# 64 bytes further: the FFN output units' split weights and the hT tiles in SBUF

## The reference

```python
def swiglu_2(h, w_in, w_out):
    a, b = jnp.split(h @ w_in, 2, axis=-1)
    return (jax.nn.silu(a) * b) @ w_out

def second_block(...):
    for l in range(DEPTH_2):
        h = rms_norm_2(x, ffn1_norm_pre[l])
        x = x + 0.5 * rms_norm_2(swiglu_2(h, ffn1_w_in[l], ffn1_w_out[l]), ffn1_norm_post[l])
        ...
        y = token_mixer(h, mem, ...)
        x = x + rms_norm_2(y, mix_norm_post[l])
        h = rms_norm_2(x, ffn2_norm_pre[l])
        x = x + 0.5 * rms_norm_2(swiglu_2(h, ffn2_w_in[l], ffn2_w_out[l]), ffn2_norm_post[l])
    return x
```

## Time and profile before

| | |
|---|---|
| median of three runs | 1726.48 us |
| the profiled execution | 1726.28 us |
| its span, first to last instruction | 1724.5 us |
| TensorE (PE) busy | 1717.4 us |
| VectorE (DVE) busy | 1072.7 us |
| ScalarE (ACT) busy | 918.9 us |
| matmuls | 12536 |
| granted clock of TensorE | full (1.00) |

### The profile page before, as it was taken

The page is one execution under the profiler, slowest core; times in us unless marked ns, Lnnn a source line. Parts: engine busy times, 40 slices in busy tenths (PEclk is TensorE's granted clock), DMA queues, the critical chain, the costliest instruction groups (busy, mean ns, idle before and its releaser), DMA issues.

```text
span 1724.5 us, 31112 instructions
## 1 busy us (share of the span) xinstructions
PE 1717.4 (100%) x12536; PEld 1586.4 (92%) x12536; DVE 1072.7 (62%) x1523; ACT 918.9 (53%) x1258; POOL 34.5 (2%) x60
## 2 busy tenths in 40 slices
PE   9999999999999999999999999999999999999998
PEld 9999888999999999999999999899999899989997
DVE  6555787655665566557677555755574667775555
ACT  6444677434454346577746444644464577664443
POOL 0000120000000000000000000000000000000000
PEclk9999999999999999999999999999999999999999
DMA  9655533655665555463355555655555553446552
GB/s 341 237 193 193 183 112 149 229 185 193 223 226 187 189 194 202 177 220 139 133 197 197 193 187 197 230 205 193 189 203 188 181 195 136 162 160 228 185 194 96
DMA packets 48415, 328.58 MB, mean 191 GB/s; under 512 B 5584, under 2 KB 5840, under 8 KB 10192
## 3 DMA queue, kind: packets, MB, share of 16 engines
q1 hardware_dynamic: 45504, 316.93, 51.3%
q10 hardware_dynamic: 2832, 10.54, 1.7%
HBM read 326.39 MB, written 1.05 MB: 190 GB/s over the span
## 4 chain that ended last, share of the span: by engine, by line
PE 99%; issue 0%; DVE 0%; ACT 0%; DVEq 0%; POOLq 0%; POOL 0%
PE work L1888 20%; PE work L1890 20%; PE work L1889 20%; PE acc L1890 8%; PE acc L1889 8%; PE acc L1888 8%; PE work L2129 4%; PE work L1993 3%; PE acc L2197 1%; PE acc L2251 1%; PE work L1978 1%; PE acc L2225 1%; PE acc L2215 0%; PE work L2379 0%; PE work L2259 0%; PE work L1950 0%
## 5 line engine op out<-in xcount | busy, mean ns | idle before, releaser
L1262 DVE TENSOR_TENSOR lo<-raw,hi 128x2048 fp32r<-128x2048 f32 x267 | 611.1, 2291 | 308.3 <-ACT hi L711 307.9
L711 ACT ACTIVATE hi<-raw 128x2048 fp32r<-128x2048 f32 x267 | 511.2, 1915 | 370.7 <-PE work L1890 346.8
L1888 PE MATMUL work<-xT_hi,hi 128*128 128x256 f32 x2464 | 685.4, 278 | 0.0
L1889 PE MATMUL work<-xT_lo,hi 128*128 128x256 f32 x2464 | 681.2, 276 | 0.0
L1890 PE MATMUL work<-xT_hi,lo 128*128 128x256 f32 x2464 | 681.1, 276 | 0.0
L1888 PEld LDWEIGHTS work<-xT_hi,hi 128*128 128x128 f32 x2464 | 462.6, 188 | 4.5 <-issue 1.7
L1889 PEld LDWEIGHTS work<-xT_lo,hi 128*128 128x128 f32 x2464 | 463.2, 188 | 2.4
L1890 PEld LDWEIGHTS work<-xT_hi,lo 128*128 128x128 f32 x2464 | 462.7, 188 | 0.0
L1890 PE MATMUL acc<-hi,hT_lo 128*128 128x512 f32 x480 | 189.1, 394 | 0.0
L1889 PE MATMUL acc<-lo,hT_hi 128*128 128x512 f32 x480 | 188.2, 392 | 0.0
L1888 PE MATMUL acc<-hi,hT_hi 128*128 128x512 f32 x480 | 186.4, 388 | 0.0
(11 more groups left out here) (357 smaller groups left out, 2108.0 us busy)
## 6 DMA issues: line engine op xcount, KB each, us to landing
raw<-stream SPq DMA_DIRECT2D x295, 1024.0 KB, 4.8
mem_in<-mem ACTq DMA_DIRECT2D x3, 1024.0 KB, 5.2
post<-post ACTq DMA_DIRECT2D x6, 512.0 KB, 4.4
raw<-stream SPq DMA_DIRECT2D x4, 512.0 KB, 9.3
memT_raw<-mem2T ACTq DMA_DIRECT2D x2, 1024.0 KB, 7.4
xT_raw<-xT SPq DMA_DIRECT2D x4, 256.0 KB, 5.4
raw<-stream SPq DMA_DIRECT2D x4, 256.0 KB, 6.0
x<-x SPq DMA_DIRECT2D x2, 512.0 KB, 9.2
```

What stands on the lines that cost most here:

```text
L711: nc.scalar.activation(dst, raw[:, s, :], ACT.Copy).then_inc(hi_ready, 1)
L1262: nc.vector.tensor_tensor(lo[:, s, :], raw[:, s, :], hi[:, s, :].bitcast(F32), ALU.subtract).then_inc(lo_ready, 1)
L1888: nc.tensor.matmul(dst, a_hi, b_hi, start=start, stop=False)
L1889: nc.tensor.matmul(dst, a_hi, b_lo, start=False, stop=False)
```

## The change

The slots of the rings `hi` and `lo` become 32 elements (128 bytes) longer. For an FFN output unit (`is_out`) the split writes its two parts 16 elements (64 bytes) further into the slot, and `out_tile` reads them there. The regions of `qT` and `probT` grow by 128 bytes, and the hT tiles in them begin 64 bytes later. The tiles behind the rings move up by multiples of 128 bytes, and `X_AT` by 512.

Afterwards, modulo 128 bytes: the input units are as before, stationary at 0 and moving at 64; in the output units the stationary operand is at 0 and the moving one at 64. The slots are now 65 times 128 bytes long, so the three slots differ modulo 256 and 512, where before they were the same. The other 512-column products keep stationary at 64 and moving at 0.

Every engine issues the same instructions in the same order as before, on the same tiles; only addresses differ.

```diff
 UNIT = 2048
 RING = 3
+OUT_SHIFT = 16
+SLOT = UNIT + 2 * OUT_SHIFT
...
-        r_hi = room(4 * RING * UNIT)
-        hi = place("hi", [P, RING, UNIT], r_hi, F32R)
-        whole = place("whole", [P, RING, UNIT], r_hi)
-        lo = new("lo", [P, RING, UNIT], F32R)
+        r_hi = room(4 * RING * SLOT)
+        hi = place("hi", [P, RING, SLOT], r_hi, F32R)
+        whole = place("whole", [P, RING, SLOT], r_hi)
+        lo = new("lo", [P, RING, SLOT], F32R)
...
-        r_qT = room(4096)
+        r_qT = room(4096 + 128)
...
-        hT_hi = place("hT_hi", [P, 2, T], r_qT, F32R)
-        hT_lo = place("hT_lo", [P, 2, T], r_qT + 2048, F32R)
+        hT_hi = place("hT_hi", [P, 2, T], r_qT + 4 * OUT_SHIFT, F32R)
+        hT_lo = place("hT_lo", [P, 2, T], r_qT + 4 * OUT_SHIFT + 2048, F32R)
...
-        r_pT = room(4096)
+        r_pT = room(4096 + 128)
...
-        hT_last = [place(f"hT_last_{part}", [P, 2, T], r_pT + 2048 * n, F32R) for n, part in enumerate(("hi", "lo"))]
+        hT_last = [place(f"hT_last_{part}", [P, 2, T], r_pT + 4 * OUT_SHIFT + 2048 * n, F32R) for n, part in enumerate(("hi", "lo"))]
...
+        def is_out(sec, n):
+
+            for base in (B1_FFN1, B1_FFN2) if sec.layer is None else (L_FFN1, L_FFN2):
+                r = n - base
+                if 0 <= r < FFN_UNITS:
+                    return r == FFN_UNITS - 1 or r % 3 == 1 and r >= 4
+            return False
+
+        def slot_of(tile, sec, n):
+
+            at = OUT_SHIFT if is_out(sec, n) else 0
+            return tile[:, sec.slot(n), at:at + UNIT]
...
-                dst = (whole if exact(sec, n) else hi)[:, s, :]
+                dst = slot_of(whole if exact(sec, n) else hi, sec, n)
...
-                nc.vector.tensor_tensor(lo[:, s, :], raw[:, s, :], hi[:, s, :].bitcast(F32), ALU.subtract).then_inc(lo_ready, 1)
+                nc.vector.tensor_tensor(slot_of(lo, sec, n), raw[:, s, :], slot_of(hi, sec, n).bitcast(F32), ALU.subtract).then_inc(lo_ready, 1)
...
-                            w = slice(D * f + 512 * c, D * f + 512 * c + 512)
+                            at = OUT_SHIFT + D * f + 512 * c
+                            w = slice(at, at + 512)
...
-X_AT = 217 * 512 + 320
+X_AT = 218 * 512 + 320
```

## The result

The change makes the kernel slower: 1734.62 us (1734.22 to 1735.08, 6 runs) beside 1726.30 us (1725.85 to 1726.56, 6 runs), a ratio of 1.0049 (95% 1.0039 to 1.0060). The profiled execution took 1734.22 us, its span is 1732.4 us, 7.9 more than before.

What follows compares the result with a forecast made beforehand. The prediction took TensorE's matmuls to bound the kernel at full clock. Output units gain 3.7 us and all other terms are zero, so 1726.48 us becomes 1722.8 us, with a range over all of 1710 to 1740 us.

Steps and rivals of the forecast that it cites:

- The output units, the term that decides: 1584 matmuls with hT and hT_last in the FFNs: 226.7 ns each instead of 229.0, 3.7 us gained.
- The carrying over per column: Output matmuls of 512 columns priced at the input units' fast pace per column, 226.7 ns.
- The term of -3.7 us: Gain forecast for the 1584 output matmuls, 2.3 ns each.
- The number forecast: An output unit's 24 matmuls should take 5.44 us instead of 5.49, start to start.
- Input units: zero: Matmuls with xT keep their residues modulo 128, so their pace and the entry behind output units stay: zero.
- some FFNs would show it and others not: What would be seen if the slots' residues modulo 256 mattered to input units behind output units; no size given.
- The rest: zero: Other tiles move by multiples of 128 bytes, and 512-column products outside the FFNs keep their old alignment: zero.
- Splits, loads and waits: Splits on ScalarE and VectorE keep 1915 and 2291 ns, loads are untouched, TensorE's waits stay near 1.2 us.
- no change: Rival: output matmuls are bound by their own 512-column stream, or only the operands' relation counts; 1726.5 us, chance 0.30.
- Slower: Rival: input units behind output units stay in the slow pace, 0.41 us a row; 1730 to 1747 us, chance 0.23.
- The independent read ports: Rule weighed: TensorE reads moving operand and weights through separate ports, so addresses can't matter and the gain is zero.
- The 215.8 ns for 512 columns: Rule weighed: columns over 2.4 GHz plus 2.5 ns for a warm matmul, giving a gain of 21 us.

Runs made afterwards that it cites:

- The swap alone: The change with slots of 8704 bytes, so all slots stand alike modulo 512, output parts and hT still shifted: 1749.70 us, ratio 1.0135.
- hT moved alone: The kernel before with hT 64 bytes further, at 128 modulo 256, rings and output parts as before: 1745.57 us, ratio 1.0112.
- The slots alone: The change without the shifted output parts and with hT in its old place, only the slots longer: 1734.34 us, ratio 1.0045.
- the parts alone at 64 and at 192: Against the kernel before, output parts 64 or 192 bytes further in 8704-byte slots, hT in its old place: 1731.09 us and 1746.34 us.

## Why the prediction was wrong

*The output units, the term that decides.* This is the step that failed first. It took the input units' pace per column, 226.7 ns, as the price of the new alignment, as if it mattered which operand starts at 64. The swap alone left 229.0: what counts is the difference of the two starts, and modulo 256, where the prediction looked modulo 128. The paces are 226.7 ns at d = 0, 229.0 at 64, 232.4 at 128, 233.3 at 192. The carrying over per column fails as well: the input units have d = 192, where 512 columns take 233.3 ns and not twice 113.3; that 226.7 is also the pace at d = 0 is luck. In the change `hi` has d = 64 and `lo` 192 in slots 0 and 2, so (2 x 229.0 + 233.3) / 3 = 230.4 ns, which is the 5.53 us of the rows after; in slot 1 it is the other way round, (2 x 233.3 + 229.0) / 3 = 231.9, and 5.54 us is 230.8, so that there the sum is about 1 ns too high. The term of -3.7 us measured +2.8. The number forecast was attainable, 5.44 us stands in the rows of hT moved alone, but by another shift.

*Input units: zero.* Wrong by 4.9 us: "same residues modulo 128" did not mean same pace. The slots alone cost these rows 4.2 us, so most of it comes with their length and not with the swap. Of the loss 4.1 us sits in FFNs 2 and 3, where the first input unit has `hi` at d = 64 and `lo` at 192 and runs at 118.9 ns. In FFN 6 it is the second input unit that has these addresses, and the pair takes its 10.91 us: so the addresses alone do not explain it. The sentence on residues modulo 256, that "some FFNs would show it and others not", is what happened.

*The rest: zero.* The 512-column products outside the FFNs were to stay as they were; the longer slots moved the weights under them, and they cost 1.4 us more. The slots' length, which the prediction did not price, makes the whole loss: the slots alone gave 1734.34 us. With the longer slots the swap adds nothing to speak of, though in slots alike modulo 512 it costs 23 us.

*What held.* Splits, loads and waits cost nothing, TensorE's sum of matmuls is the time, and the clock was full. Of the rivals, "no change" had the reason right (only the relation of the operands counts) for the swap's pace, and the time wrong. "Slower" had the place right and came in part; the swap alone shows it whole, with its price: 0.40 us a row more than before, where 0.41 was given. That the measured time lies in its range is in part luck, since 4.2 of the 7.9 us came from 512-column products, which it did not name.

*The rules weighed.* The independent read ports of the Trainium skill (SBUF — State Buffer, "Who interferes with whom") do not fit what TensorE does here: one and the same matmul takes 226.7 to 233.3 ns by the difference of its two operands' starts, and the measurement decides. The 215.8 ns for 512 columns are what the Trainium skill (TensorE: Matmul & The Clock Gate, "Back-to-back issue gap") gives as the gap of a single isolated matmul, and not of a row with a weight load for each, as here. That pace was reached at none of the addresses tried; the best unit stands at 226.7.

*What stays open.* Why a row of input units enters one pace or the other. Rows at the same d in both kinds of units are fast in the kernel before and slow with the swap alone, and one kernel had fast and slow FFNs in one execution; in the kernel before, two output units at d = 64 behind a slow row took 11.20 us for 48 products, 233.3 ns each, from the 1266.10 of the earlier trace rows to this line:

```profile
1277.30 0.28 PE L1888 MATMUL work<-memT_hi,hi 128*128 128x256 f32 x1
```

So d gives the pace in a clean row, and there is a second, lasting one beside it. What lies ahead of the row bears on the entry: kernels with the input units' operands at the same addresses, to the byte, enter fast or slow by where the output units' operands lie (before and hT alone; the parts alone at 64 and at 192). In the two kernels with `hi` at 192 and `lo` at 64 in every slot (`lo` 128 bytes further, with d = 64/192 and with d = 0 in the output units) none of 50 rows lost over 0.06 us; in the change it is the other way round in slot 1, and FFNs 2 and 3 have units at 118.9 ns there. That the 192/64 mix protects is the rule that this suggests, not a cause that was shown. One of the twelve executions of the kernel before that stand beside hT alone took 1730.70 us, 4 us over their median; an FFN of nine slow rows would cost 3.6, but no trace of it was kept.

## What to carry to other kernels

Where matmuls follow each other without a gap, write down the starts of both operands modulo 256 before moving a tile, the ring's slot length included: a slot that is an odd multiple of 128 bytes gives neighbouring slots different residues. Try moves one tile at a time, read the pace from starts (of a unit, and of the row behind it), and look at all rows behind the one that was improved: here the faster output units cost over seven times their gain (20.0 us for 2.8) in the input units behind them. Where rows have two lasting paces, several executions are needed: one kernel here spread from 1726.30 to 1735.86 us.

## What was not expected of the hardware

Four paces of one 512-column fp32r product by d modulo 256, 226.7, 229.0, 232.4 and 233.3 ns, in clean rows the same for hT, memT and merged wherever two of them stood at one d. Two lasting paces of the 256-column products at one d = 192, 113.3 and 117.7 ns, which hold for 96 matmuls and, across output units, for whole FFNs; 120.0 at d = 0.
